# A two-block transformer on one core: bias and maximum in one instruction, rotation in head pairs between weight slots, a new order in the pooling stage

## What is computed

```python
def first_block(x, ...):
    ...
    sw = jnp.einsum('bqgrd,bkgd->bgrqk', qc, kwc) * scale + bias_w
    p_w = masked_softmax(sw, mask_w)
    ...
def second_block(x, c, ...):
    ...
    x = x + 0.5 * (1.0 + g) * swiglu(h, ffn_w_in[layer, 0], ffn_w_out[layer, 0])
    if layer < N_A_LAYERS:
        y = pool_mixer(h, pool_w[layer], pool_scale[layer])
    else:
        q = rope(rms_norm_2((h @ w_q[j]).reshape(B, T, 8, 128), q_norm[j]), cos, sin)
        y = moba_attention(q, k_blocks, v_blocks, k_mean) @ w_o[j]
    x = x + (1.0 + g) * y
    x = x + 0.5 * (1.0 + g) * swiglu(h, ffn_w_in[layer, 1], ffn_w_out[layer, 1])
    ...
    k = rope(rms_norm_2(k, k_norm), cos, sin)     # keys and values once, after layer 0
```

## Time and profile before

| | |
|---|---|
| median of 3 runs | 1463.04 us (1459.38 to 1464.31) |
| the profiled execution | 1458.97 us, its span 1457.2 us |
| busy in the span | PE 1392.0, DVE 954.0, ACT 661.3 us |
| mean granted TensorE clock | 0.968 |

### The profile page before, as it was taken

The page is one execution under the profiler, slowest core; times in us unless marked ns, Lnnn a source line. Parts: engine busy times, 40 slices in busy tenths (PEclk is TensorE's granted clock), DMA queues, the critical chain, the costliest instruction groups (busy, mean ns, idle before and its releaser), DMA issues.

```text
span 1457.2 us, 16672 instructions
## 1 busy us (share of the span) xinstructions
PE 1392.0 (96%) x6765; PEld 1131.9 (78%) x6765; DVE 954.0 (65%) x1063; ACT 661.3 (45%) x862; POOL 24.6 (2%) x48
## 2 busy tenths in 40 slices
PE   7998998899999899998999999989999996999998
PEld 6986566688888688887888888868888884788887
DVE  3448875866667866667876667575666758654544
ACT  4445544654444634344543445543334545544342
POOL 2200000000000000000000000000000000000000
PEclk8998898999999999999999999999999999999999
DMA  8888625767777488785387784557787531265551
GB/s 241 221 266 230 186 98 191 273 234 274 278 286 256 166 293 297 260 305 199 115 316 278 262 312 145 182 172 259 258 287 284 190 135 40 87 202 189 186 188 72
DMA packets 165568, 317.55 MB, mean 218 GB/s; under 512 B 7018, under 2 KB 114852, under 8 KB 156276
## 3 DMA queue, kind: packets, MB, share of 16 engines
q1 hardware_dynamic: 161872, 305.50, 61.4%
q0 software_dynamic: 3440, 10.93, 2.8%
q10 hardware_dynamic: 180, 0.05, 0.0%
HBM read 314.10 MB, written 1.84 MB: 217 GB/s over the span
## 4 chain that ended last, share of the span: by engine, by line
PE 85%; DVE 9%; ACT 3%; issue 2%; DMA 1%; SPq 0%; ACTq 0%; DVEq 0%
PE bank L688 25%; PE bank L690 25%; PE bank L689 25%; PE bank L783 2%; DVE full L1685 1%; DMA raw<-in_w_in 1%; PE bank L708 1%; PE bank L991 1%; DVE wlo L1618 1%; PE bank L711 1%; DVE acc L1605 1%; ACT whi L1248 1%; PE bank L982 1%; PE bank L735 1%; DVE xt L1673 1%
## 5 line engine op out<-in xcount | busy, mean ns | idle before, releaser
L1618 DVE TENSOR_TENSOR wlo<-raw,whi 128x2048 fp32r<-128x2048 f32 x205 | 469.2, 2290 | 282.5 <-ACT whi L1248 282.2
L1248 ACT ACTIVATE whi<-raw 128x2048 fp32r<-128x2048 f32 x205 | 392.0, 1913 | 208.3 <-PE bank L690 201.4
L688 PE MATMUL bank<-whi,uhi 128*128 128x512 f32 (+2 forms) x1088 | 431.6, 397 | 13.8 <-DVE mix L1936 3.8
L690 PE MATMUL bank<-whi,ulo 128*128 128x512 f32 (+2 forms) x1088 | 421.0, 387 | 0.0
L689 PE MATMUL bank<-wlo,uhi 128*128 128x512 f32 (+2 forms) x1088 | 420.3, 386 | 0.0
L688 PEld LDWEIGHTS bank<-whi,uhi 128*128 128x128 f32 x1088 | 207.2, 190 | 60.4 <-issue 14.0
L690 PEld LDWEIGHTS bank<-whi,ulo 128*128 128x128 f32 x1088 | 206.9, 190 | 42.4
L689 PEld LDWEIGHTS bank<-wlo,uhi 128*128 128x128 f32 x1088 | 207.6, 191 | 39.8 <-issue 1.3
L688 PE MATMUL bank<-whi,hsplit 128*128 128x512 f32 (+1 forms) x512 | 202.2, 395 | 2.1 <-DVE hsplit L1762 2.1
L689 PE MATMUL bank<-wlo,hsplit 128*128 128x512 f32 (+1 forms) x512 | 199.7, 390 | 0.0
L690 PE MATMUL bank<-whi,hsplit 128*128 128x512 f32 (+1 forms) x512 | 199.7, 390 | 0.0
(11 more groups left out here) (236 smaller groups left out, 1104.0 us busy)
## 6 DMA issues: line engine op xcount, KB each, us to landing
raw<-in_ffn_w_in SPq DMA_DIRECT2D x176, 512.0 KB, 4.8
ada<-in_ada_w SPq DMA_DIRECT2D x72, 1024.0 KB, 7.2
raw<-in_ffn_w_out SPq DMA_DIRECT2D x44, 1024.0 KB, 5.0
raw<-in_w_in SPq DMA_DIRECT2D x16, 1024.0 KB, 8.3
raw<-in_w_mlp_in SPq DMA_DIRECT2D x16, 1024.0 KB, 6.7
raw<-in_w_mlp_out SPq DMA_DIRECT2D x16, 1024.0 KB, 4.9
ada<-in_kv_ada_w SPq DMA_DIRECT2D x8, 1024.0 KB, 7.8
raw<-in_w_kv SPq DMA_DIRECT2D x8, 1024.0 KB, 5.2
```

What stands on the lines that cost most here:

```text
L688: nc.tensor.matmul(o, sh, mh, start=start, stop=False, skip_group_check=skip)
L690: return nc.tensor.matmul(o, sl, mh, start=False, stop=stop, skip_group_check=skip)
L1248: ins = nc.scalar.activation(whi[:, ring(n), :], raw[:, ring(n), :], ACT.Copy)
L1618: ins = nc.vector.tensor_tensor(wlo[:, ring(n), :], raw[:, ring(n), :], whi[:, ring(n), :].bitcast(F32), ALU.subtract)
```

## The change

Four things change, and no arithmetic besides how the bias and the maximum are formed. (1) In an attention unit, the two additions and two maxima on DVE become two instructions that do both. (2) The sums, roots, swaps and rotations of a head pair are issued one or two slots after the pair's own slot, in `kv` and in `wq`; the last two pairs of queries are rotated between the first attention units, and `ffn2` no longer starts with 40 unused transposes. (3) In `pool`, DVE forms the input of the first half before it adds the second half, and PE joins the halves after the product of the first; 16 unused transposes are put ahead. (4) 18 unused transposes are put at the start of `ffn0`, and four pieces of adaptive vectors move by one place.

```diff
-  ((3, 1), ((19, None, 7, 8), (8, 0, 4, 0))),
-  ((4, 0), ((8, 1, 5, 0),)),
-  ((4, 1), ((17, 0, 6, 0),)),
-  (("ffn1", 3), ((17, 1, 7, 0),)),
+  ((3, 1), ((19, None, 7, 8),)),
+  ((4, 0), ((8, 0, 4, 0),)),
+  ((4, 1), ((8, 1, 5, 0),)),
+  (("ffn1", 3), ((17, 0, 7, 0),)),
+  (("ffn1", 5), ((17, 1, 7, 0),)),
...
   window(e, 0)
+  if e == 2:
+      keep_busy(18, bank[5])
   turn_u(e, 0)
...   (PE, ffn2)
   pe.wait_ge(v2_taken, 2)
-  keep_busy(40, bank[4])
-  pe.wait_ge(v2_taken, 4)
   pe.wait_ge(u2_lo, 1)
...
+  if i == 1 and name == "ffn2":
+      pe.wait_ge(v2_taken, 4)
   turn_h(p0 + i - 1, c0 + i - 1, hf2, 0)
...   (PE, pool)
   pe.wait_ge(pool_in, 32)
+  keep_busy(16, bank[7])
   windows(0, 0)
   windows(0, 1)
   window(3, 0)
-  windows_across()
   pe.wait_ge(lo_done, n + 1)
   pooled(0)
+  windows_across()
...   (PE, kv)
   for q in range(4):
       pe.wait_ge(u2_full, q + 1)
       wide8(b + 2 + q, bank[q])
+      if q > 1:
+          swap_halves(0, q - 2)
+      if q > 0:
+          head_sums(0, q - 1)
   u_slot(b + 6, 0, bank[6:8])
-  head_sums(0)
+  swap_halves(0, 2)
+  head_sums(0, 3)
   u_slot(b + 7, 1, bank[6:8])
-  swap_halves(0)
+  swap_halves(0, 3)
...   (PE, wq)
   wide8(b + q, bank[q], u_at=24 if q == 0 else None)
-  head_sums(1)
-  swap_halves(1)
+      if q > 1:
+          swap_halves(1, q - 2)
+      if q > 0:
+          head_sums(1, q - 1)
+  head_sums(1, 3)
+  def last_heads(u):          # after the step of unit u
+      if u < 2:
+          swap_halves(1, 2 + u)
...   (ACT, kv; wq is alike, with conv(b + 6) after the last root)
   rotary_copy(0, q, ...)
   conv(b + 5 + q)
+  if q:
+      rotary_root(0, q - 1)
...
   u2_high(0)
-  rotary_root(0)
   conv(b + 9)
-  act.wait_ge(pe_done, b + 8)
+  rotary_root(0, 3)
+  conv(b + 10)
   u2_high(1)
   nc.scalar.preload_act_table_set(SILU)
   take_v(1)
-  conv(b + 10)
...   (DVE, an attention unit)
-  nc.vector.tensor_tensor(pr[:, 0:P], bank[...][:, 0:P], b[:, P:T], ALU.add)
-  link(nc.vector.tensor_tensor(pr[:, P:384], bank[...][:, P:384], b, ALU.add))
-  nc.vector.tensor_reduce(sm[:, 6:7], pr[:, 0:P], AX.X, ALU.max)
-  link(nc.vector.tensor_reduce(sm[:, 7:8], pr[:, P:384], AX.X, ALU.max))
+  nc.vector.tensor_tensor_reduce(pr[:, 0:P], bank[...][:, 0:P], b[:, P:T], 1.0, LEAST,
+                                 ALU.add, ALU.max, sm[:, 6:7])
+  link(nc.vector.tensor_tensor_reduce(pr[:, P:384], bank[...][:, P:384], b, 1.0, LEAST,
+                                      ALU.add, ALU.max, sm[:, 7:8]))
...   (DVE, pool)
   conv(n + 1)
+  pool_input(0)
   add_half(3, 1)
-  pool_input(0)
   pool_low(0)
...   (DVE, kv)
-  for n in range(b + 3, b + 9):
+  for n in range(b + 3, b + 7):
       conv(n)
+  rotary(0, 0, tmp2, k2, k2)
+  conv(b + 7)
+  rotary(0, 1, tmp2, k2, k2)
+  conv(b + 8)
   u2_low(0)
+  rotary(0, 2, tmp2, k2, k2)
   conv(b + 9)
+  conv(b + 10)
   u2_low(1)
-  conv(b + 10)
-  rotary(0, tmp2, k2, k2)
+  rotary(0, 3, tmp2, k2, k2)
...   (DVE, wq)
   for q in range(4):
-      conv(b + 3 + q)
+      if q > 1:
+          rotary(1, q - 2, q2, tmp2, q2)
+      if q < 3:
+          conv(b + 3 + q)
       take_piece(b + q)
-  rotary(1, q2, tmp2, q2)
   def between_second(u):
+      if u in (0, 2):
+          rotary(1, 2 + u // 2, q2, tmp2, q2)
+      if u == 3:
+          conv(b + 6)
```

More of the change, by code:

```diff
@@ L137 @@
 BIAS_COPIES = 32
+LEAST = -3.0e38
 VEC = {"mix_pre": 0, "mix_post": 8, "mlp_pre": 16, "mlp_post": 24, "norm_g": 32, "pool_scale": 80,
@@ L1166, in _, with head_sums, swap_halves @@
             ffn("ffn1", 4)
[L1168 to L1179, removed]
+            def head_sums(r, q):
+                pe.wait_ge(r_copy, 8 * r + 2 * q + 2)
+                nc.tensor.matmul(bank[q][:, :], ones, hroot[r][:, 2 * q:2 * q + 2, :], start=True,
+                                 stop=True).then_inc(r_ss, 1)
+            def swap_halves(r, q):
+                pe.wait_ge(r_root, 4 * r + q + 1)
+                src = q2 if r else tmp2
+                nc.tensor.matmul(bank[q][:, :], const("swap"), src[:, 2 * q:2 * q + 2, :], start=True,
+                                 stop=True).then_inc(r_swap, 1)
             b = START["kv"]
@@ L1214, in _ @@
                       lambda u: bank[u // 2][:, (u % 2) * T:(u % 2 + 1) * T],
-                      lambda u: None, lambda u: True, lambda u: True)
+                      lambda u: None, lambda u: True, lambda u: True, last_heads)
             for q in range(4):
@@ L1526, in rotary_copy, with rotary_root @@
                 nc.scalar.activation(hroot[r][:, 2 * q:2 * q + 2, :], bank[q][:], ACT.Square).then_inc(r_copy, 1)
[L1528 to L1533, removed]
+            def rotary_root(r, q):
+                act.wait_ge(r_ss, 4 * r + q + 1)
+                h = hroot[r][:, 2 * q:2 * q + 2, :]
+                link(nc.scalar.activation(h, bank[q][:], ACT.Ln, bias=eps[:], scale=1.0 / P))
+                nc.scalar.activation(h, h, ACT.Exp, scale=-0.5).then_inc(r_root, 1)
             def take_v(c):
@@ L1567, in _ @@
                 rotary_copy(1, q, scal[:, QSC, 0:1], q2)
-                conv(b + 3 + q)
-            rotary_root(1)
+                if q:
+                    rotary_root(1, q - 1)
+                if q < 3:
+                    conv(b + 3 + q)
+            rotary_root(1, 3)
+            conv(b + 6)
             def o_between(u):
@@ L1830, in attention @@
                         b = bias_of(u)
-                        nc.vector.tensor_tensor(pr[:, 0:P], bank[4 + w % 2][:, 0:P], b[:, P:T], ALU.add)
-                        link(nc.vector.tensor_tensor(pr[:, P:384], bank[4 + w % 2][:, P:384], b, ALU.add))
-                        nc.vector.tensor_reduce(sm[:, 6:7], pr[:, 0:P], AX.X, ALU.max)
-                        link(nc.vector.tensor_reduce(sm[:, 7:8], pr[:, P:384], AX.X, ALU.max))
+                        nc.vector.tensor_tensor_reduce(pr[:, 0:P], bank[4 + w % 2][:, 0:P], b[:, P:T], 1.0, LEAST,
+                                                       ALU.add, ALU.max, sm[:, 6:7])
+                        link(nc.vector.tensor_tensor_reduce(pr[:, P:384], bank[4 + w % 2][:, P:384], b, 1.0, LEAST,
+                                                            ALU.add, ALU.max, sm[:, 7:8]))
                         if sink_of(u) is not None:
@@ L1999, in _, with rotary @@
             dve.wait_ge(rotary_in, 16)
[L2001 to L2010, removed]
+            def rotary(r, q, src, turned, dst):
+                s = slice(2 * q, 2 * q + 2)
+                dve.wait_ge(r_root, 4 * r + q + 1)
+                dve.wait_ge(r_swap, 4 * r + q + 1)
+                nc.vector.tensor_tensor(src[:, s, :], src[:, s, :], cos, ALU.mult)
+                link(nc.vector.tensor_tensor(turned[:, s, :], bank[q][:].rearrange("p (a b) -> p a b", a=2), sin, ALU.mult))
+                link(nc.vector.tensor_tensor(dst[:, s, :], src[:, s, :], turned[:, s, :], ALU.add))
+                nc.vector.tensor_tensor(dst[:, s, :], dst[:, s, :], hroot[r][:, s, :], ALU.mult).then_inc(r_done, 1)
             def u2_low(c):
```

## The result

The changed kernel takes **1439.61 us** in the median (1433.67 to 1442.49, 4 runs), against 1461.54 us for the kernel before on the same chip (1459.38 to 1464.31, 4 runs): a ratio of 0.9844, 95% interval 0.9806 to 0.9882. That is 1.6% faster. Forecast were 1437 us and 1427 to 1450. The profiled execution took 1438.23 us, with a span of 1436.4 us and a mean granted clock of 0.973. I read it in the order of the prediction.

What follows compares the result with a forecast made beforehand. PE, busy 96% of the span, was taken as the bound, its largest waits being for DVE. Terms -7 - 7 - 5 - 1.7 - 3 = -23.7 from 1458.97 gave 1435, set to 1437 us; range 1427 to 1450.

Steps and rivals of the forecast that it cites:

- The fused instruction: Attention units on DVE: bias and maxima take 0.85 us instead of 1.30, saving 0.45 a unit.
- Rival (a): Fusing gives nothing and the rest works: 1444 us, bounds 1440 to 1450; chance 0.2.
- Queries and the second attention: Rotations moved between slots and units, with fusing, end the second attention at 1230.5, not 1237.5: -7 us.
- Keys in kv and ffn2: Rotations by pairs inside kv and no 40 transposes start ffn2 earlier: -7 us, from -5 to -8.
- The new wait: At the start of ffn2, PE waits 0.5 us for u2_low after its first slot.
- the wait for the hidden product: In ffn2, part 0's product is taken about 1.2 us after PE is done, in place of 3.75.
- First attention: Shorter DVE units shrink PE's gaps and avoid some slow clock: -5 us, from 0 to -11.
- the two falls: Slow-clock stretches after PE gaps in the first attention; one taken as avoided, at half effect: -3 us.
- pool: Pooling stage: first half's input formed earlier, halves joined behind the product: -3 us, from 0 to -5.
- ffn0: Start of ffn0: 18 transposes fill a wait of 3.02 and keep the clock up: -1.7 us, 0 to -2.2.
- I don't add all of it: Whole kernel: profiled execution was 4.1 us below the median, so 1437 us was forecast against 1435 from that execution.
- Rival (b): New orders only exchange waits, other parts worth half, fusing as forecast: 1450 to 1459 us; chance 0.1.

Runs made afterwards that it cites:

- e1: The kernel before with only the fused bias-and-maximum instructions: 1460.51 us, ratio 0.9969.
- e9: The changed kernel with the two additions and two maxima of a unit as four instructions again: 1449.06 us, ratio 0.9914.
- e2: The kernel before with only the rotations by head pairs in kv and wq, and without the 40 transposes: 1453.28 us, ratio 0.9923.
- e4: The changed kernel without the 18 new transposes at ffn0 and the 16 in pool: 1442.13 us, ratio 0.9843.
- e5: The changed kernel with ACT rounding pool's first half before squaring the second: 1439.25 us, ratio 0.9836.
- e7: The changed kernel with pool's old order on DVE and PE, new transposes and moved pieces kept: 1444.66 us, one execution.
- e10: The changed kernel with the 40 unused transposes put back ahead of ffn2's first product: 1442.32 us, ratio 0.9871.
- e3: The kernel before with only pool's new order, the moved pieces and the 16 and 18 new transposes: 1462.06 us, ratio 0.9993.
- e6: The changed kernel with 31 more unused transposes in PE's gaps of the first attention: 1431.84 us, ratio 0.9791.
- e8: The changed kernel with the edits of e5 and e6 together: 1427.01 us, ratio 0.9763.

## Why the prediction was right, step by step

**The total** (1437 against 1439.6) was right in its direction and in most of its mechanisms, but that it came so close is in part luck: the second attention won more by the fused instruction and less by the moves than forecast, `pool` won less, and of the span's 20.8 us the low clock of the trace of before at the entry of `wq` gave 1.6.

**The fused instruction: the mechanism right, two terms mis-sized.** "I take 0.85 a unit, a saving of 0.45": it measured 0.67 and 0.63, the lower bound. And "0.45 to 0.64 comes off two units and not off one: 2.0 a unit" failed. It was read from a unit of the old loop with a DVE wait of 0.17. In the old order it roughly held: from the first unit to the eighth e1 saves 2.4 us, 0.34 a unit, though PE's clock was 0.66 from 1220 to 1230 there, against 0.88 before, and the runs don't part the loop from the clock. In the new order DVE nearly always has work, so each unit gives all of its 0.63: 5.0 us in the stage (e9 against the change: -4.0 and -9.0) where I had 2.5. Rival (a), that fusing gives nothing, fell: e9 is that case, at 1449.06.

The Trainium skill (VectorE: DVE Perf Modes, section Two Vector instructions with no wait between them) counts an instruction with an accumulator output as two, and the trace agrees, with a read record of 0.08 us. Its section Rules for kernel authors advises against fusing chained operations for speed; that doesn't hold here, since the second of the two is a small read and not a pass over the tile. The two fused operations with their reads took 0.67 us, four operations 1.30.

**Queries and the second attention: -7 forecast, -9.0 found, of which -7.4 without the low clock of the trace of before at the entry of `wq`.** Without it the moves alone gave -3.0 (e2) and -2.3 (e9), where I had -4.5, and the fused instruction added 5.0 where I had 2.5. That the sum comes so near to -7 is two errors that offset each other. PE's waits for probabilities went up by 1.8, against 7.3 that went.

**Keys in kv and ffn2: -7 forecast, -7.6 (e2) and -6.3 (the change) found.** The new wait is 0.4 (0.5 forecast), the wait for the hidden product 1.3 (1.2 forecast). The 40 transposes are 3.7 (4.3 less the new wait, 3.8, forecast). The two numbers differ by a loss of clock at the entry of `kv`: in the change, the two stretches from 890 to 910 had 0.91, where before had 1.00, and DVE comes 1.2 us later to the second half of the norm ahead of `kv`. e2 has none of this loss; without it the change would have -7.5 too.

**First attention: -5 forecast, -4.1 found, for another reason.** "I take one of the two falls as avoided" failed: neither was (0.56 and 0.54 in the rows above). The gaps shrank as expected (2.23 to 1.41 at the first), and that only shortened the first fall. What was won is the fused instruction's: e9 without it has +0.1. But its size is uncertain, and -4.1 is the luckiest of six traces in which this stage is the same: the others (e1, e4, e5, e7, e10) have -1.1 to -3.9, the mean is -2.6. The four traces without the instruction (before, e2, e3, e9) have 0 to +3.9, mean +1.4, so it was worth about 4 between the means. What the avoided falls are worth e6 shows: 6.7 us more than the change by stage, 7.8 by the medians; e8 has the same -10.8.

**pool: -3 forecast, -0.5 found** (-1.4 and +0.9 in `ffn1`). This is the term that failed. I had seen that ACT squares the second half before it rounds, and put `u_lo` "about 0.9 us earlier"; counted from the stage's start it was 0.3. And I let the clock and the shorter PE path bring 2 more, while the product hung on ACT alone. Behind the wait of 2.82 the clock was low again (0.66 from 680 to 690), which the forecast had named as a possibility: "the clock may fall again, and then under 1 is left". e4 shows that the clock costs nothing ahead of that wait, e5 that ACT's order was worth 2.7. The moved piece I said "comes back later" and gave no price; it is the 0.9.

**ffn0: -1.7 forecast, -1.4 found** in every trace with the transposes. But e1 and e4, which lack them, show -0.9, and e2, which lacks them too, 0.0: the same gap of 3.02 cost less clock in the first two. The part is worth 0.5 to 1.4, and the runs can't tell it from nothing (e3, e4).

**The clock.** "I don't add all of it" of the 4.1 us that the profiled execution lay below the median was sound: the change's profiled execution lay 1.4 below its own. Run to run, the kernels spread over 2 us (e6) to 11 (e4), and e1 shows two groups. The Trainium skill (TensorE: Matmul & The Clock Gate, section What's actually happening) says that the number of slow matmuls at the start of one and the same kernel varies from run to run. In these runs the mean clock of whole executions varies: e1's twelve have 0.961 to 0.974. No run here shows several starts of one kernel.

**Two sums of the forecast were wrong.** Rival (b), half of 7, 4.5, 1.7 and 3 with fusing as forecast (7.5), makes 15.6 off 1458.97 or off the median, 1443 to 1447, and not 1450 to 1459. And the range to 1450 leaves out all of the stated 1450 to 1459, not half. Neither touches the forecast itself.

Multiplied, the parts alone give 0.9969 x 0.9923 x 0.9993 = 0.9885, just above the upper edge of the whole's interval. The stages suggest that fusing is worth more when the rotations sit on DVE's path (3.0 alone, which is e1's 4.6 less the 1.6 at the entry of `wq`, and 5.0 within, in the second attention) and that e1's median carries a loss of clock. How much each adds can't be settled from one trace per kernel.

## What to carry to other kernels

Ask of each term which engine's queue ends last at that place after the change, not before it: a saving on an engine that has become the pace setter counts in every turn of the loop, and a saving ahead of another engine's late work counts nothing. Unused transposes pay where PE's work behind the gap is PE-bound (first attention, 31 of them for 7 to 8 us) and bring nothing where PE waits for DVE or ACT anyway (second attention, `pool`, the 40 in `ffn2`, which cost 3.7). Where the clock moves in single executions, a part worth less than a few us is read from stages in several traces, not from medians.

## What the hardware showed unexpectedly

- An addition and a running maximum in one DVE instruction take as long as the addition (0.28 us for 128x128, 0.42 for 128x256, scores read from PSUM). Each is followed by a read of the accumulator of 0.08 us, most of it hidden: the pair with both reads takes 0.67 us, two plain additions 0.66.
- Shrinking the gap ahead of a fall of the clock from 2.23 to 1.41 us didn't avoid the fall; filling it and the next one with 13 transposes did.
- The same gap of 3.02 us, ahead of the same work, was followed by four records of 3.62 us in two traces (before, e2), and of 2.53 and 2.52 in two others (e1, e4); with the gap filled they took 1.88.
